# RWKV scan: inclusive decay sums only, decay products of both directions in one instruction, turned and unit blocks copied by ScalarE and GpSimd

## The chip, the cores and the metric

One Trainium2 chip, one of its cores. The metric is the device time in microseconds of one execution. The kernel before has a median of 3497.85 us over 3 runs (3496.07 to 3501.37). All data are float32; large products are made from high and low parts.

## The reference

Two transformer blocks of width 1024 on 1024 tokens. The first mixes with an RWKV-7 scan and a gated linear attention (GLA), each over half of the width, then an FFN and an embedding gate; the second mixes with neighbourhood attention and a convolution, then an MLP. The change is in the RWKV scan, which for each of 8 heads of 64 channels goes once forwards and once backwards over the tokens:

```python
def rwkv7_scan(r, decay, k, v, kk, b, reverse):
    def step(S, inp):                      # S: 64 x 64 for each head
        r_t, w_t, k_t, v_t, kk_t, b_t = inp
        sa = jnp.einsum('bhij,bhj->bhi', S, -kk_t)
        S = (S * w_t[:, :, None, :] + sa[..., None] * b_t[:, :, None, :]
             + v_t[..., None] * k_t[:, :, None, :])
        return S, jnp.einsum('bhij,bhj->bhi', S, r_t)
    ...
# decay = exp(-exp(-softplus(...) - 0.5)), that is exp(-exp(-0.5) * sigmoid(...))
y = (rwkv7_scan(r_h, heads(decay[:, :, 0]), k_h, v_h, kk, b_h, False)
     + rwkv7_scan(r_h, heads(decay[:, :, 1]), k_h, v_h, kk, b_h, True))
```

## The kernel before, in words

The program is written out engine by engine: each stage has one method per engine (`..._pe`, `..._act`, `..._dve`, `..._pool`, `..._sp`), each engine runs its instructions in the order written, and `wait_ge` makes an engine wait for a named count of another engine or of a transfer. Nothing is planned by a scheduler: the order in the methods is the order on the engines. `dve.c` stands for VectorE after a wait for its own last instruction.

The scan cuts the 1024 tokens into 16 chunks of 64 (NSUB), 8 blocks of two chunks (NBLK). A step handles one chunk of the forward direction (d = 0) and one of the backward direction (d = 1) at the same time, 4 pairs of heads each: 8 lanes, two heads on the two halves of the partitions. Within a chunk the recurrence is turned into products of matrices, for which a 64x64 triangular matrix has to be inverted for every head.

All engines run a loop over u from -2 to 15, software-pipelined: iteration u finishes chunk u, inverts for chunk m = u + 1 and prepares chunk n = u + 2, and VectorE makes the decay products of chunk u + 3. The pieces, by name:
- cum (TensorE, L1493): sums of the log decay of a block as a product with the constant `tri`, for even u up to 10. For every lane it gives 128 inclusive and 128 exclusive sums, in PSUM banks 2 and 3 of each direction; bank 2 also holds the right sides, bank 3 also ss.
- exps (ScalarE, L1609 to L1611): Ex, En and Ei, the exponentials of the exclusive sums, of the negative inclusive and of the inclusive sums.
- products (VectorE, L1700 to L1705), six instructions for each direction: F (the decay from chunk to chunk), AR and BK (kk, b, r and k times their decays), and the last decay kept for the next F.
- gb, gk (TensorE): the Gram matrices of BK and AR; masked into NM and MM by VectorE (L1720). tr (L1560): BK turned, copied to BKT by ScalarE (L1632).
- The inverse. VectorE inverts the 16x16 diagonal blocks by substitution in 15 steps on 32 partitions (`substitute_dve`, L1676 and L1677). NM goes to DRAM and its blocks come back as N16 (SP and GpSimd queues, L1427). Z16 holds the inverse at [:, :, 1], started as unit blocks (`identity_dve`, L1655) and turned to [:, :, 0] at the end (L1679, its mark is `x16`). Z16 goes to DRAM (L1459) and comes back as block diagonals ZZ: even blocks by SP, odd ones by GpSimd (L1436). Two levels then merge the blocks: p4 with ZZ, T (L1743), l4 (L1586, L1587), ZZ2 (L1747), p5, T (L1751), l5, XT (L1757). Of substitution n, steps 0 to 3 stand ahead of XT and steps 4 to 14 behind it.
- rh (`right_sides_pe`), copied with its sign changed to Rn by ScalarE (L1620); uu = XT times Rn, copied to U by ScalarE (L1623); ss and yy: the new state S and the output, both of which use U. VectorE adds ss into S (L1715) and scales it (L1725). y is written by ScalarE for u < 8 (L1628) and added by VectorE from then on (L1731).

In iterations with sums, rh stands behind l5, elsewhere ahead of p4. SP's order in its iteration n: NM to DRAM, ZZ blocks of n - 1, N16 blocks of n, the next sigmoids, Z16 to DRAM. GpSimd's: ZZ blocks of n - 1, N16 blocks of n. The helper that issues most of the products has one line (L1484), so a product is known by its tiles: ps<-s_AR,s_BK is gb or gk, ps<-s_ZZ,s_NM is p4, ps<-s_Rn,s_XT is uu.

Of the kernel before, what the change touches and what calls it, by code (L numbers as in the profile page):

```python
# [44 lines left out]
def constants():  # L45
# [6 lines left out]
    tri = np.zeros((2, PART, 2, PART), f)  # L52
    s, q = t[:, None], t[None, :]
    for d, (inc, exc) in enumerate((((s <= q), (s < q)), ((s >= q), (s > q)))):
        tri[d, :, 0] = DECAY * np.where(same, inc.astype(f) - 0.5, 0)
        tri[d, :, 1] = DECAY * np.where(same, exc.astype(f) - 0.5, 0)
    c["tri"] = np.ascontiguousarray(tri.transpose(1, 0, 2, 3)).reshape(PART, -1)
# [154 lines left out]
class Kernel:  # L212
# [116 lines left out]
    def plan_block1(self):  # L329
# [74 lines left out]
        self.tri, self.gram_mask, self.lev_mask = sb("tri", [PART, 2, 2 * PART]), sb("gram_mask", [PART, 2, 2, CH]), sb("lev_mask", [PART, 2, 2, CH])  # L404
        self.sig = sb("sig", [PART, 2, RW])
        self.Ei, self.En, self.Ex = (sb(n, [PART, LANES, PART]) for n in ("s_Ei", "s_En", "s_Ex"))
# [1032 lines left out]
    def rwkv_scan_sp(self):  # L1439
        sp, sg, pe, dve = self.sp, self.dram["sg"], self.pe, self.dve  # L1440
# [7 lines left out]
        for n in range(NSUB):  # L1448
# [9 lines left out]
            sp.wait_ge(dve["x16", n])  # L1458
# [5 lines left out]
        sp.wait_ge(dve["pr", NSUB - 1, 1])  # L1464
# [22 lines left out]
    def cum_pe(self, t):  # L1487

        pe = self.pe
        pe.wait_ge(self.t_in["sig", t])  # L1490
        for d in range(2):
            for x in range(4):
                mm = pe.e.matmul(self.ps[:, 4 * d + 2 + x // 2, (x % 2) * 256:(x % 2) * 256 + 256], self.sig[:, d, blk(x)], self.tri[:, d, :],  # L1493
                                 start=True, stop=True)
            mm.then_inc(*pe.one("cum", t, d))

    def right_sides_pe(self, u):
# [4 lines left out]
        for d in range(2):  # L1502
            pe.wait_ge(dve["scaled", u, d], self.pool["zero"])
            if (u % 2 or u == 0) and (u + 3) // 2 < NBLK:
                pe.wait_ge(act["Ei", (u + 3) // 2, d])
            elif u:
                pe.wait_ge(act["U", u - 1, d])
            if u:
                pe.wait_ge(self.yes(u - 1)["y", u - 1, d])
# [7 lines left out]
    def rwkv_scan_pe(self):  # L1517
        pe, act, dve, ps = self.pe, self.act, self.dve, self.ps
        for u in range(-2, NSUB):
# [6 lines left out]
            if n < NSUB:  # L1526
                AR_n = self.AR[n % 3]
                for w, name in ((0, "gb"), (1, "gk")):
                    for d in range(2):
                        pe.wait_ge(dve["pr", n, d])  # L1530
# [13 lines left out]
            elif u >= 0:  # L1544
                for d in range(2):
                    pe.wait_ge(act["U", u, d])
                    if u:
                        pe.wait_ge(dve["S", u - 1, d])
                    self.heads_pe(d, 3, CH, 0, ((lambda l, H: BKT[H, l, 1, :], v), (lambda l, H: BKT[H, l, 0, :], lambda l, H: self.U[H, l, :])), "ss", u, d)
# [13 lines left out]
            if sums:  # L1563
                if u >= 0:
                    pe.wait_ge(act["U", u, 1], self.yes(u)["y", u, 1], dve["S", u, 1])
                else:
                    pe.wait_ge(act["Ei", 0, 1])
                self.cum_pe((u + 4) // 2)
            elif 0 <= m < NSUB:
                self.right_sides_pe(m)  # L1570
            if 0 <= m < NSUB:
# [24 lines left out]
                if sums and m > 0:  # L1596
                    self.right_sides_pe(m)
        self.meet(pe, "rwkv_scan")

    def exps_act(self, t):  # L1600
# [3 lines left out]
        for d in range(2):  # L1604
            cum = ps[:, 4 * d + 2:4 * d + 4, :].rearrange("p b (l x t) -> p (b l) x t", l=2, x=2)
            act.wait_ge(pe["cum", t, d])
            if t:
                act.wait_ge(dve["pr", 2 * t - 1, d])
            act.e.activation(self.Ex[:, L[d]], cum[:, :, 1, :], ACTF.Exp).then_inc(*act.one())  # L1609
            act.e.activation(self.En[:, L[d]], cum[:, :, 0, :], ACTF.Exp, scale=-1.0).then_inc(*act.one())  # L1610
            act.e.activation(self.Ei[:, L[d]], cum[:, :, 0, :], ACTF.Exp).then_inc(*act.one("Ei", t, d))  # L1611

    def rwkv_scan_act(self):
        pe, act, dve, ps = self.pe, self.act, self.dve, self.ps
        L = [slice(0, 4), slice(4, 8)]
        for u in range(-2, NSUB):
            if u >= 0:
                for d in range(2):
                    act.wait_ge(pe["rh", u, d])
                    act.e.activation(self.Rn[:, L[d]], self.hb(d, 2), ACTF.Copy, scale=-1.0).then_inc(*act.one("Rn", u, d))  # L1620
                for d in range(2):
# [16 lines left out]
    def rwkv_scan_pool(self):  # L1638
        pool = self.pool
        pool.e.memset(self.S[0][:], 0.0).then_inc(*pool.one("zero"))  # L1640
        for n in range(NSUB + 1):
# [3 lines left out]
            if n < NSUB:  # L1645
                pool.wait_ge(self.t_n["out", n])
                self.blocks_there(pool, self.t_nb, n, range(5, 8))
        self.meet(self.pool, "rwkv_scan")

    def identity_dve(self, n):  # L1650

        dve = self.dve
        if n:
            dve.wait_ge(self.t_z["out", n - 1])
        dve.c.tensor_copy(self.Z16[:, :, 1], self.eye16[:]).then_inc(*dve.one("one", n))  # L1655

    def substitute_dve(self, n, first, end):
# [3 lines left out]
        if first == 0:  # L1661
            dve.wait_ge(dve["one", n])
# [6 lines left out]
        for s in range(first, end):  # L1669
# [7 lines left out]
            dve.c.tensor_tensor(rows, rows, part, ALU.subtract).then_inc(*dve.one())  # L1677
        if end == 15:
            dve.c.tensor_copy(self.Z16[:, :, 0], self.Z16[:, :, 1].rearrange("p d i c -> p d c i")).then_inc(*dve.one("x16", n))  # L1679

    def rwkv_scan_dve(self):
# [8 lines left out]
        def products(n, d):  # L1690
            t, AR, F = n // 2, self.AR[n % 3], self.F[n % 3]
            tok, s = self.gla_where(t, n % 2)[d]
            tc, W = slice(s * CH, (s + 1) * CH), slice(tok, tok + CH)
            last = s * CH + (CH - 1 if d == 0 else 0)
            dve.wait_ge(act["Ei", t, d])
            if n >= 3:
                dve.wait_ge(pe["yy", n - 3, d])
            if n:
                dve.wait_ge(pe["tr", n - 1, d])
            dve.c.tensor_tensor(F[:, L[d]], self.last[:, L[d]], self.Ei[:, L[d], last:last + 1], ALU.mult).then_inc(*dve.one())  # L1700
            dve.e.tensor_tensor(AR[:, L[d], 0], self.kk[:, :, W], self.Ex[:, L[d], tc], ALU.mult).then_inc(*dve.one())
# [1547 lines left out]
```

## Time and profile before

| | |
|---|---|
| median of 3 runs | 3497.85 us |
| profiled execution | 3500.24 us, its span 3498.9 us |
| scan, from the end of its second substitution to the end of its last | 752.1 to 1075.6 us of the span |
| TensorE busy | 3207.0 us, 92% |
| VectorE busy | 2220.8 us, 63% |
| ScalarE busy | 980.7 us, 28% |
| GpSimd busy | 459.9 us, 13% |
| granted TensorE clock, mean | 0.953 |

Busy time is the time in which an engine has an instruction at work; waits, semaphore and DMA-issuing instructions don't count. Matmuls overlap each other, and a row of a timeline joins like instructions that follow each other. The granted clock has two levels, 1.00 (2.4 GHz) and 0.50 (1.2 GHz). "Idle before <-releaser" is the time an engine stood still ahead of an instruction and what ended it.

### The profile page before, as it was taken

To read this page: it belongs to the slowest core of one execution; us is meant where nothing else is said; L and a number is where in the kernel's file an instruction comes from. 1 tells how busy PE (TensorE), PEld (TensorE's weight loads), DVE (VectorE), ACT (ScalarE), POOL (GpSimd) and SP (SyncE) were. 2 spreads that over 40 slices of the span, in tenths; PEclk is the share of its full clock that TensorE was granted. 3 is DMA by queue.
4 is the path that set the end of the run, shared out by engine and by line. 5 is a ranking of instruction groups with operands and counts; after the bars stand their busy time and mean duration, and the time that the engine had idled before them with its cause. 6 is when DMAs were issued, how large, how long until landed. Compare 5 with 4: busy or idle time off the path is not lost.

```text
span 3498.9 us, 58647 instructions
## 1 busy us (share of the span) xinstructions
PE 3207.0 (92%) x25755; PEld 2639.0 (75%) x25755; DVE 2220.8 (63%) x3060; ACT 980.7 (28%) x1514; POOL 459.9 (13%) x357
## 2 busy tenths in 40 slices
PE   6988888989987989999999887998998799999996
PEld 4777767778886878888888676885667688888885
DVE  4757655778886544444444566997546566666666
ACT  4544224322213221111111444112563211111112
POOL 2530023422224000000000121000001011111110
PEclk9988788999998999999999999999999899999999
DMA  4410044322224021111111212113001111111111
GB/s 128 127 63 11 20 134 139 118 40 42 40 31 171 7 67 37 55 55 37 55 55 42 80 42 73 49 43 99 2 2 61 42 49 49 49 49 49 49 49 66
DMA packets 242727, 207.41 MB, mean 59 GB/s; under 512 B 66744, under 2 KB 205127, under 8 KB 241959
## 3 DMA queue, kind: packets, MB, share of 16 engines
q1 hardware_dynamic: 223527, 176.96, 17.0%
q10 hardware_dynamic: 13824, 25.17, 2.3%
q0 software_dynamic: 5120, 1.53, 0.5%
q8 instruction: 202, 3.31, 0.4%
q14 instruction: 54, 0.44, 0.0%
HBM read 172.06 MB, written 29.64 MB: 58 GB/s over the span
## 4 chain that ended last, share of the span: by engine, by line
PE 69%; DVE 18%; ACT 5%; POOL 2%; DMA 2%; issue 2%; SPq 1%; ACTq 0%; DVEq 0%; POOLq 0%
PE ps L2176 23%; PE ps L2191 17%; PE ps L2038 5%; PE ps L640 3%; PE ps L641 3%; PE ps L642 3%; DVE Yc L2801 2%; PE ps L2900 2%; DVE s_tmp L1676 2%; DVE s_Z L1677 2%; PE ps L1484 1%; POOL a_x L2551 1%; PE ps L2926 1%; PE ps L2916 1%; PE ps L1012 1%
## 5 line engine op out<-in xcount | busy, mean ns | idle before, releaser
L3205 DVE TENSOR_TENSOR H<-H,ps 128x1024 f32<-128x1024 f32 x256 | 312.7, 1221 | 181.5 <-PE ps L2191 174.5
L2341 DVE TENSOR_TENSOR fsum<-fsum,ps 128x1024 f32<-128x1024 f32 x168 | 205.2, 1221 | 312.4 <-PE ps L2191 310.1
L2191 PE MATMUL ps<-dh,hh 128*128 128x512 f32 x864 | 340.1, 394 | 19.8 <-DVE hl L2156 13.9
L2191 PE MATMUL ps<-dl,hh 128*128 128x512 f32 x864 | 338.7, 392 | 0.0
L2191 PE MATMUL ps<-dh,hl 128*128 128x512 f32 x864 | 338.7, 392 | 0.0
L2176 PE MATMUL ps<-hn_h,uh 128*128 128x512 f32 x704 | 275.9, 392 | 7.2 <-DVE ul L1786 4.7
L2176 PE MATMUL ps<-hn_h,ul 128*128 128x512 f32 x704 | 275.4, 391 | 0.0
L2176 PE MATMUL ps<-hn_l,uh 128*128 128x512 f32 x704 | 275.4, 391 | 0.0
L2176 PE MATMUL ps<-hx_h,uh 128*128 128x512 f32 x512 | 201.4, 393 | 7.8 <-DVE hx_l L2156 5.3
L2191 PEld LDWEIGHTS ps<-dh,hh 128*128 128x128 f32 x864 | 163.9, 190 | 57.9 <-DVE hl L2156 15.5
L2176 PE MATMUL ps<-hx_h,ul 128*128 128x512 f32 x512 | 201.0, 393 | 0.0
L2176 PE MATMUL ps<-hx_l,uh 128*128 128x512 f32 x512 | 201.0, 393 | 0.0
L2191 PEld LDWEIGHTS ps<-dh,hl 128*128 128x128 f32 x864 | 163.7, 189 | 34.3
L2191 PEld LDWEIGHTS ps<-dl,hh 128*128 128x128 f32 x864 | 163.8, 190 | 33.7
L2551 POOL TENSOR_TENSOR a_x<-a_x,a_t 128x512 f32<-128x512 f32 x84 | 128.9, 1534 | 336.9 <-ACT a_t L2540 334.5
L3175 POOL TENSOR_TENSOR dw<-dw,g_row 128x1024 f32<-128x1024 f32 x32 | 78.7, 2461 | 708.5 <-DMA dw<-in_w_mlp_dram 708.5
L2176 PEld LDWEIGHTS ps<-hn_h,uh 128*128 128x128 f32 x704 | 133.1, 189 | 35.5 <-DVE ul L1786 5.2
L2801 DVE SCALAR_TENSOR_TENSOR Yc<-cp,cols,Yc 128x1024 f32<-128x1024 f32 x120 | 154.2, 1285 | 4.3
L2176 PEld LDWEIGHTS ps<-hn_l,uh 128*128 128x128 f32 x704 | 133.2, 189 | 27.7
L2176 PEld LDWEIGHTS ps<-hn_h,ul 128*128 128x128 f32 x704 | 133.0, 189 | 27.8
L3184 ACT ACTIVATE relu<-ps 128x1024 f32<-128x1024 f32 x32 | 32.9, 1030 | 404.4 <-PE ps L2176 404.4
L640 PE MATMUL ps<-hx_h,cw 128*128 128x512 f32 x320 | 129.7, 405 | 18.1 <-DVE cw L620 8.4
(473 smaller groups left out, 7412.3 us busy)
## 6 DMA issues: line engine op xcount, KB each, us to landing
aw<-in_w_ada_dram ACTq DMA_DIRECT2D x96, 256.0 KB, 3.0
uw<-in_w_mlp_dram SPq DMA_DIRECT2D x32, 512.0 KB, 4.4
dw<-in_w_mlp_dram SPq DMA_DIRECT2D x32, 512.0 KB, 5.2
uw<-in_ffn_gate_dram SPq DMA_DIRECT2D x22, 512.0 KB, 4.0
uw<-in_ffn_up_dram SPq DMA_DIRECT2D x22, 512.0 KB, 5.3
dw<-in_ffn_down_dram SPq DMA_DIRECT2D x22, 512.0 KB, 6.0
cw<-in_w_in_dram SPq DMA_DIRECT2D x20, 512.0 KB, 3.8
o_w<-in_w_out_dram SPq DMA_DIRECT2D x16, 512.0 KB, 10.0
```

The source lines that it names most:

```text
L640: pe.e.matmul(ps[0:m, 2 * (j % 2) + h, :], wh[:, k, :], xh, start=(k == 0), stop=False)
L641: pe.e.matmul(ps[0:m, 2 * (j % 2) + h, :], wh[:, k, :], xl, start=False, stop=False)
L642: mm = pe.e.matmul(ps[0:m, 2 * (j % 2) + h, :], wl[:, k, :], xh, start=False, stop=(k == kc - 1))
L1676: dve.c.tensor_tensor(part, col, pivot, ALU.mult).then_inc(*dve.one())
L2038: mm = pe.e.matmul(self.ps[:, 2 * (t % 2) + hf, :], x[a](k), w[b](k)[:, half(hf)], start=(n == 0 and m == 0), stop=(n == len(order) - 1 an ...
L2176: mm = pe.e.matmul(ps[:, 2 * pair + h, :], w[:, col], x[h][v][:, k, :], start=(k == 0 and m == 0), stop=(k == DC - 1 and m == 2))
L2191: mm = pe.e.matmul(ps[:, 2 * pair + hf, :], v[s][:, blk(t)], w[:, half(hf)], start=(m == 0), stop=(m == 2))
L2341: return dve.c.tensor_tensor(f, f, new, ALU.add) if g else dve.c.tensor_copy(f, new)
L2551: pool.c.tensor_tensor(acc[:], acc[:], self.a_t[who][:], ALU.add).then_inc(*pool.one("ada", q, who))
L2801: dve.c.scalar_tensor_tensor(out=o, in0=x[:, w:w + TOK], scalar=self.col("dw", n + 4 * w), in1=o, op0=ALU.mult, op1=ALU.add) \
L3175: pool.e.tensor_tensor(w, w, self.g2_row[:], ALU.mult).then_inc(*pool.one("m", "dw", g))
L3205: return dve.c.tensor_tensor(h, h, self.ps[:, 4 + 2 * (t % 2):6 + 2 * (t % 2), :], ALU.add)
```

## The change

- The exclusive sums are no longer computed: `tri` keeps 128 columns for each direction, cum fills bank 3 alone. The exclusive decay is the inclusive one of the token before: the exponentials go to a tile Eb of 65 columns for each chunk, with one edge column exp(-end) added. Ei and Ex are two views of Eb, shifted by one. ScalarE still has three activations for each direction, one of them with 8 columns.
- The products of both directions are made by one set of six instructions of 512 columns. The set waits for both directions' exps, yy and tr. Marks `pr` lose their direction.
- The turned copy of Z16 moves from VectorE to ScalarE (mark `x16`), between the Rn copies and the U copies of iteration u, for chunk u + 1; it waits for VectorE's mark `z16`, set by the last substitution step. The unit blocks move to GpSimd (mark `one`), between its ZZ and its N16 transfers.
- rh stands ahead of p4 in every iteration, and its wait for the exps (bank 2) goes to ss (bank 3). cum waits for S alone.

```diff
@@ -49,12 +49,8 @@
...
-    tri = np.zeros((2, PART, 2, PART), f)
     s, q = t[:, None], t[None, :]
-    for d, (inc, exc) in enumerate((((s <= q), (s < q)), ((s >= q), (s > q)))):
-        tri[d, :, 0] = DECAY * np.where(same, inc.astype(f) - 0.5, 0)
-        tri[d, :, 1] = DECAY * np.where(same, exc.astype(f) - 0.5, 0)
-    c["tri"] = np.ascontiguousarray(tri.transpose(1, 0, 2, 3)).reshape(PART, -1)
+    c["tri"] = np.concatenate([DECAY * np.where(same, inc.astype(f) - 0.5, 0) for inc in (s <= q, s >= q)], 1).astype(f)
@@ -401,9 +397,9 @@
...
         self.room = self.r0 + 112 * 1024
-        self.tri, self.gram_mask, self.lev_mask = sb("tri", [PART, 2, 2 * PART]), sb("gram_mask", [PART, 2, 2, CH]), sb("lev_mask", [PART, 2, 2, CH])
+        self.tri, self.gram_mask, self.lev_mask = sb("tri", [PART, 2, PART]), sb("gram_mask", [PART, 2, 2, CH]), sb("lev_mask", [PART, 2, 2, CH])
         self.sig = sb("sig", [PART, 2, RW])
-        self.Ei, self.En, self.Ex = (sb(n, [PART, LANES, PART]) for n in ("s_Ei", "s_En", "s_Ex"))
+        self.En, self.Eb = sb("s_En", [PART, LANES, 2, CH]), sb("s_Eb", [PART, LANES, 2, CH + 1])
@@ -1455,13 +1451,13 @@
...
                 sig((n + 3) // 2)
-            sp.wait_ge(dve["x16", n])
+            sp.wait_ge(act["x16", n])
             sp.e.dma_start(zd[n % 2].rearrange("k x d w i c -> (k x) (d w i c)"), self.Z16[:].rearrange("p d w i c -> p (d w i c)")) \
...
@@ -1490,8 +1486,7 @@
...
             for x in range(4):
-                mm = pe.e.matmul(self.ps[:, 4 * d + 2 + x // 2, (x % 2) * 256:(x % 2) * 256 + 256], self.sig[:, d, blk(x)], self.tri[:, d, :],
-                                 start=True, stop=True)
+                mm = pe.e.matmul(self.ps[:, 4 * d + 3, blk(x)], self.sig[:, d, blk(x)], self.tri[:, d, :], start=True, stop=True)
             mm.then_inc(*pe.one("cum", t, d))
@@ -1501,12 +1496,8 @@
...
             pe.wait_ge(dve["scaled", u, d], self.pool["zero"])
-            if (u % 2 or u == 0) and (u + 3) // 2 < NBLK:
-                pe.wait_ge(act["Ei", (u + 3) // 2, d])
-            elif u:
-                pe.wait_ge(act["U", u - 1, d])
             if u:
-                pe.wait_ge(self.yes(u - 1)["y", u - 1, d])
+                pe.wait_ge(act["U", u - 1, d], self.yes(u - 1)["y", u - 1, d])
             self.heads_pe(d, 2, CH, 0, ((lambda l, H: MM[H, l, 0, :], lambda l, H: self.VT[H, tok[l // 4], l % 4, :]),
@@ -1527,7 +1518,7 @@
...
                     for d in range(2):
-                        pe.wait_ge(dve["pr", n, d])
+                        pe.wait_ge(dve["pr", n])
                         if u >= 0:
@@ -1546,6 +1537,10 @@
...
                         pe.wait_ge(dve["S", u - 1, d])
+                    if u % 2 and (u + 3) // 2 < NBLK:
+                        pe.wait_ge(act["Ei", (u + 3) // 2, d])
+                    elif u == 0:
+                        pe.wait_ge(act["Ei", 1, d])
                     self.heads_pe(d, 3, CH, 0, ((lambda l, H: BKT[H, l, 1, :], v), (lambda l, H: BKT[H, l, 0, :], lambda l, H: self.U[H, l, :])), "ss", u, d)
@@ -1561,12 +1556,9 @@
...
             if sums:
-                if u >= 0:
-                    pe.wait_ge(act["U", u, 1], self.yes(u)["y", u, 1], dve["S", u, 1])
-                else:
-                    pe.wait_ge(act["Ei", 0, 1])
+                pe.wait_ge(dve["S", u, 1] if u >= 0 else act["Ei", 0, 1])
                 self.cum_pe((u + 4) // 2)
-            elif 0 <= m < NSUB:
+            if 0 <= m < NSUB:
                 self.right_sides_pe(m)
@@ -1593,8 +1585,6 @@
...
                     self.heads_pe(d, 1, CH, 0, ((lambda l, H: self.T[H, l, :], lambda l, H: ZZ2[H, l, 1, :]),), "l5", m, d)
-                if sums and m > 0:
-                    self.right_sides_pe(m)
         self.meet(pe, "rwkv_scan")
@@ -1602,13 +1592,14 @@
...
         for d in range(2):
-            cum = ps[:, 4 * d + 2:4 * d + 4, :].rearrange("p b (l x t) -> p (b l) x t", l=2, x=2)
+            cum = ps[:, 4 * d + 3, :].rearrange("p (l s t) -> p l s t", l=4, s=2)
+            inc, edge, end = (slice(1, CH + 1), slice(0, CH))[d], (slice(0, 1), slice(CH, CH + 1))[d], (slice(CH - 1, CH), slice(0, 1))[d]
             act.wait_ge(pe["cum", t, d])
             if t:
-                act.wait_ge(dve["pr", 2 * t - 1, d])
-            act.e.activation(self.Ex[:, L[d]], cum[:, :, 1, :], ACTF.Exp).then_inc(*act.one())
-            act.e.activation(self.En[:, L[d]], cum[:, :, 0, :], ACTF.Exp, scale=-1.0).then_inc(*act.one())
-            act.e.activation(self.Ei[:, L[d]], cum[:, :, 0, :], ACTF.Exp).then_inc(*act.one("Ei", t, d))
+                act.wait_ge(dve["pr", 2 * t - 1])
+            act.e.activation(self.Eb[:, L[d], :, inc], cum, ACTF.Exp).then_inc(*act.one())
+            act.e.activation(self.Eb[:, L[d], :, edge], cum[:, :, :, end], ACTF.Exp, scale=-1.0).then_inc(*act.one())
+            act.e.activation(self.En[:, L[d]], cum, ACTF.Exp, scale=-1.0).then_inc(*act.one("Ei", t, d))
@@ -1618,6 +1609,10 @@
...
                     act.e.activation(self.Rn[:, L[d]], self.hb(d, 2), ACTF.Copy, scale=-1.0).then_inc(*act.one("Rn", u, d))
+            if 0 <= u + 1 < NSUB:
+                act.wait_ge(dve["z16", u + 1])
+                act.e.activation(self.Z16[:, :, 0], self.Z16[:, :, 1].rearrange("p d i c -> p d c i"), ACTF.Copy).then_inc(*act.one("x16", u + 1))
+            if u >= 0:
                 for d in range(2):
@@ -1643,23 +1638,18 @@
...
             if n < NSUB:
+                pool.wait_ge(self.t_misc["r_const"])
+                pool.e.tensor_copy(self.Z16[:, :, 1], self.eye16[:]).then_inc(*pool.one("one", n))
                 pool.wait_ge(self.t_n["out", n])
...
-    def identity_dve(self, n):
-        dve = self.dve
-        if n:
-            dve.wait_ge(self.t_z["out", n - 1])
-        dve.c.tensor_copy(self.Z16[:, :, 1], self.eye16[:]).then_inc(*dve.one("one", n))
     def substitute_dve(self, n, first, end):
...
         if first == 0:
-            dve.wait_ge(dve["one", n])
+            dve.wait_ge(self.pool["one", n])
             dve.wait_ge(self.t_n["in", n], self.t_nb["in", n])
@@ -1674,9 +1664,7 @@
...
             dve.c.tensor_tensor(part, col, pivot, ALU.mult).then_inc(*dve.one())
-            dve.c.tensor_tensor(rows, rows, part, ALU.subtract).then_inc(*dve.one())
-        if end == 15:
-            dve.c.tensor_copy(self.Z16[:, :, 0], self.Z16[:, :, 1].rearrange("p d i c -> p d c i")).then_inc(*dve.one("x16", n))
+            dve.c.tensor_tensor(rows, rows, part, ALU.subtract).then_inc(*(dve.one("z16", n) if s == 14 else dve.one()))
@@ -1687,25 +1675,35 @@
...
-        def products(n, d):
-            t, AR, F = n // 2, self.AR[n % 3], self.F[n % 3]
-            tok, s = self.gla_where(t, n % 2)[d]
-            tc, W = slice(s * CH, (s + 1) * CH), slice(tok, tok + CH)
-            last = s * CH + (CH - 1 if d == 0 else 0)
-            dve.wait_ge(act["Ei", t, d])
+        def both(x, y):
+            return bass.AP(tensor=x.tensor, offset=x.offset, ap=[x.ap[0], [y.offset - x.offset, 2]] + list(x.ap[1:]))
+        def products(n):
+            t, AR, BK, F = n // 2, self.AR[n % 3], self.BK, self.F[n % 3]
+            (tok, s), (tok_b, s_b) = self.gla_where(t, n % 2)
+            W, W_b = slice(tok, tok + CH), slice(tok_b, tok_b + CH)
+            def decays(at, at_b):
+                return both(self.Eb[:, L[0], s, at:at + CH], self.Eb[:, L[1], s_b, at_b:at_b + CH])
+            def lanes(x):
+                return x.rearrange("p (d x) t -> p d x t", d=2)
+            Ei, Ex, En = decays(1, 0), decays(0, 1), both(self.En[:, L[0], s], self.En[:, L[1], s_b])
+            end = both(self.Eb[:, L[0], s, CH:CH + 1], self.Eb[:, L[1], s_b, 0:1])
+            dve.wait_ge(act["Ei", t, 0], act["Ei", t, 1])
             if n >= 3:
-                dve.wait_ge(pe["yy", n - 3, d])
+                dve.wait_ge(pe["yy", n - 3, 1])
             if n:
-                dve.wait_ge(pe["tr", n - 1, d])
-            dve.c.tensor_tensor(F[:, L[d]], self.last[:, L[d]], self.Ei[:, L[d], last:last + 1], ALU.mult).then_inc(*dve.one())
-            dve.e.tensor_tensor(AR[:, L[d], 0], self.kk[:, :, W], self.Ex[:, L[d], tc], ALU.mult).then_inc(*dve.one())
-            dve.e.tensor_tensor(self.BK[:, L[d], 0], self.bb[:, :, W], self.En[:, L[d], tc], ALU.mult).then_inc(*dve.one())
-            dve.e.tensor_tensor(AR[:, L[d], 1], rkv[:, 0:4, W], self.Ei[:, L[d], tc], ALU.mult).then_inc(*dve.one())
-            dve.e.tensor_tensor(self.BK[:, L[d], 1], rkv[:, 4:8, W], self.En[:, L[d], tc], ALU.mult).then_inc(*dve.one())
-            dve.c.tensor_copy(self.last[:, L[d]], self.Ei[:, L[d], last:last + 1]).then_inc(*dve.one("pr", n, d))
-        for d in range(2):
-            products(0, d)
+                dve.wait_ge(pe["tr", n - 1, 1])
+            dve.c.tensor_tensor(lanes(F[:]), lanes(self.last[:]), end, ALU.mult).then_inc(*dve.one())
+            dve.e.tensor_tensor(lanes(AR[:, :, 0]), both(self.kk[:, :, W], self.kk[:, :, W_b]), Ex, ALU.mult).then_inc(*dve.one())
+            dve.e.tensor_tensor(lanes(BK[:, :, 0]), both(self.bb[:, :, W], self.bb[:, :, W_b]), En, ALU.mult).then_inc(*dve.one())
+            dve.e.tensor_tensor(lanes(AR[:, :, 1]), both(rkv[:, 0:4, W], rkv[:, 0:4, W_b]), Ei, ALU.mult).then_inc(*dve.one())
+            dve.e.tensor_tensor(lanes(BK[:, :, 1]), both(rkv[:, 4:8, W], rkv[:, 4:8, W_b]), En, ALU.mult).then_inc(*dve.one())
+            dve.c.tensor_copy(lanes(self.last[:]), end).then_inc(*dve.one("pr", n))
+        products(0)
         for u in range(-2, NSUB):
@@ -1732,11 +1730,8 @@
...
                     self.rwkv_rk_dve(c)
-            for d in range(2):
-                if u + 3 < NSUB:
-                    products(u + 3, d)
-            if n < NSUB:
-                self.identity_dve(n)
+            if u + 3 < NSUB:
+                products(u + 3)
             if 0 <= m < NSUB:
```

## Rows read from the trace of the kernel before

**Rows 1.** The page: span, and each engine's busy time, share and instructions.

```profile
span 3498.9 us, 58647 instructions
...
PE 3207.0 (92%) x25755; PEld 2639.0 (75%) x25755; DVE 2220.8 (63%) x3060; ACT 980.7 (28%) x1514; POOL 459.9 (13%) x357
```

**Rows 2.** Windows, core 0: stretch, length, busy of PE, PEld, DVE, ACT, POOL, clock, DMA.

```profile
752.10:1075.60 323.50, 293.18 (x7694) 276.69 (x7689) 266.53 (x841) 63.22 (x136) 83.96 (x140) 0.98 0.22 37
870.80:872.70 1.90, 0.09 (x4) 0.03 (x2) 1.75 (x7) 0.38 (x1) 1.90 (x4) 1.00 0.26 19
873.40:876.70 3.30, 3.30 (x68) 3.30 (x64) 1.54 (x3) 0.00 (x0) 0.00 (x0) 0.50 0.63 164
```

**Rows 3.** Chain of waits, 700 to 1100: start us, length us, what.

```profile
752.13 0.60 DVE s_Z L1679
...
888.33 0.61 DVE s_Z L1679
...
891.30 0.53 SPq L1436
...
897.07 0.71 PE ps L1484 x16
...
911.44 0.62 DVE s_Z L1679
...
1075.59 0.58 DVE s_Z L1679
...
1078.29 4.78 DVE r_rkv L1917 x4
1083.08 0.44 DVE s_T L1743
```

**Rows 4.** PE's waits, 752.1 to 1075.6: us in total, times, longest.

```profile
PE ps L1484 <- DMA s_ZZ<-zd_dram: 14.3, 11, 2.2
```

**Rows 5.** Timeline of ScalarE: start, length, instruction, [idle before <-releaser].

```profile
748.02 0.85 ACT L1623 ACTIVATE s_U<-ps 128x256 f32<-128x256 f32 x2 [10.13 <-PE ps L1484]
...
884.22 0.85 ACT L1623 ACTIVATE s_U<-ps 128x256 f32<-128x256 f32 x2 [12.94 <-PE ps L1484]
...
908.99 0.85 ACT L1623 ACTIVATE s_U<-ps 128x256 f32<-128x256 f32 x2 [3.58 <-PE ps L1484]
...
914.51 0.38 ACT L1628 ACTIVATE B<-ps 128x256 f32<-128x256 f32 x1 [1.02 <-PE ps L1484]
...
916.38 0.60 ACT L1632 ACTIVATE s_BKT<-ps 128x512 f32<-128x512 f32 x1 [0.34 <-PE ps L1560]
...
918.24 0.38 ACT L1620 ACTIVATE s_Rn<-ps 128x256 f32<-128x256 f32 x1 [0.55 <-PE ps L1484]
...
1069.82 0.85 ACT L1623 ACTIVATE s_U<-ps 128x256 f32<-128x256 f32 x2 [11.21 <-PE ps L1484]
```

**Rows 6.** Timeline of TensorE.

```profile
872.67 0.51 PE L1484 MATMUL ps<-s_ZZ,s_NM 64*64 64x64 f32 x10 [1.81 <-DMA s_ZZ<-zd_dram]
...
892.27 3.72 PE L1493 MATMUL ps<-tri,sig 128*128 128x256 f32 x16
```

**Rows 7.** Timeline of VectorE.

```profile
881.28 0.73 DVE L1757 TENSOR_TENSOR s_XT<-s_ZZ,ps 128x256 f32<-128x256 f32 x2
...
889.53 1.27 DVE L1720 TENSOR_TENSOR s_NM<-ps,gram_mask 128x512 f32<-128x512 f32 x2
...
892.80 0.17 DVE L1700 TENSOR_TENSOR s_F<-s_last,s_Ei 128x4 f32<-128x4 f32 x1
...
896.43 0.41 DVE L1655 COPY s_Z<-eye 32x512 f32<-32x512 f32 x1
```

**Rows 8.** Groups by line and form, GpSimd, whole span: xcount | busy us, mean ns | idle.

```profile
L2551 POOL TENSOR_TENSOR a_x<-a_x,a_t 128x512 f32<-128x512 f32 x84 | 128.9, 1534 | 336.9 <-ACT a_t L2540 334.5
...
L1640 POOL MEMSET s_S<- 128x512 f32 x1 | 0.5, 524 | 11.8 <-DVE s_last L1685 11.8
```

More of the change, by code:

```diff
@@ L1439, in rwkv_scan_sp @@
     def rwkv_scan_sp(self):
-        sp, sg, pe, dve = self.sp, self.dram["sg"], self.pe, self.dve
+        sp, sg, pe, act, dve = self.sp, self.dram["sg"], self.pe, self.act, self.dve
         nd, zd = self.dram["nd"], self.dram["zd"]
@@ L1463, in rwkv_scan_sp @@
         i = self.i
-        sp.wait_ge(dve["pr", NSUB - 1, 1])
+        sp.wait_ge(dve["pr", NSUB - 1])
         for dst, src in ((self.r_hones[:], i["k_head_ones"]), (self.r_hsel2[:], i["k_head_sel"]), (self.r_gup[:], i["rwkv_g_up"][0]),
```

## The prediction

> **What bounds the kernel now.** I read the page first: TensorE is busy 92% of the span and VectorE 63% [rows 1]. These shares are averages over stages, so next came a stretch of the scan alone, between the ends of its second and last substitution: in 323.5 us TensorE is busy 293, VectorE 267, ScalarE 63 [rows 2]. Neither of the first two is saturated, so the step is set by a loop, and I took the chain of waits to see it [rows 3]. I mark a step by E, the start of the copy at L1679, which is the end of the 15 substitution steps. From E = 888.33 VectorE copies (L1679), adds S, masks NM; the SP queue issues the return of the inverted blocks at 891.30; p4 (the first product with ZZ) starts at 897.07, so 8.7 us after E; from there p4, T, l4, ZZ2, p5, T, l5, XT and eleven substitution steps reach the next E at 911.44, 14.37 us later. The first marked E is 752.13, the last 1075.59: 14 periods of 23.1 us [rows 3]. TensorE's waits for the returned blocks are only 14.3 us over the stage [rows 4]: transfer, VectorE's filling work and TensorE end almost together, so taking work from one of them can give little, and holding one of them up costs at once.
>
> ScalarE looks free (63 us of 323), but what matters is when its few instructions are due. U of the step is copied at 884.22, 4.1 us before E, and in the steps with decay sums at 908.99, 2.4 us before E; the first U is at 748.02 (E 752.13), the fifteenth at 1069.82 (E 1075.59) [rows 3, 5]. U comes before E in every step.
>
> **The change, part by part.**
>
> *The turned copy goes to ScalarE, and this is the term that decides.* In the new ScalarE program of iteration u the order is Rn(u), turn x16(u+1), U(u). The turn waits for z16(u+1). VectorE's iteration u-1 ends with substitution n = u+1, so z16(u+1) is exactly the E ahead of which U(u) is copied now. ScalarE takes its instructions in order: U(u) can't start until E. Queued behind U(u) are ss(u) and yy(u) on TensorE (L1549 and the line of yy behind it), behind them tr(u+2), the sums, the right sides and p4; and on VectorE S(u) waits for ss(u), with NM, MM, products and all transfers of the next step behind it. Fifteen U (u = 0 to 14) are held.
>
> I place the new step from E on. ScalarE sees E 0.1 us later. The 32x512 turn: 0.60 us is what a 128x512 activation takes (the BKT row), the 128x256 ones take 0.38, VectorE needed 0.61 for this copy [rows 3, 5]; bounds 0.4 to 1.1 (twice the 512-column row, less overlap, for its strided read); I take 0.5 until the next one issues, so U starts at E+0.6. From a U, the rows of 908.99 to 918.24 give what TensorE does with no wait: second y copy 5.52 later, second BKT 7.39, second Rn 9.25 [rows 5]. So tr is done at E+8.0 and the right sides at E+9.85.
> - Steps with sums (u = 0, 2, ... 10: six). The sums take 3.72 us now for 16 matmuls of 256 columns [rows 6]; with 128 columns between 1.86 and 3.72, I take 1.86, as time per matmul here goes with columns. The right sides now stand ahead of p4 in these steps too. p4 at 9.85 + 1.86 = E+11.7.
> - Steps without (eight of the fourteen periods). TensorE is ready at E+9.85, and the returned blocks decide. ss is two fifths of the matmuls between U and the second y copy, so about 0.45 + 2.0 us: S of the second direction starts at E+3.0, NM is done 0.33 + 1.2 later [rows 7], E+4.5. SP sends NM first and then its half of the ZZ blocks, so the issue at 891.30 (E+3.0 now) moves to E+5.0; now p4 follows that issue by 5.77 us [rows 3], in other steps by 5.0. p4 at E+10.0 to 10.8; I take 10.6.
> From p4 to the next E nothing is changed: 14.37. Periods at full clock: 26.1 and 25.0. Six and eight of them: 356.6 us against 323.5, so **+33**. The last step: y of both directions now waits for U(14), E+6.5, and L1917 (4.78 us) follows: T at E+11.4 where it was 1083.08 - 1075.59 = E+7.5; +3.9, with the clock below **+4.8**.
>
> *TensorE's clock.* From the end of uu (the second of the two U copies of 884.22 starts about 3.7 us before E) to E+1.05 TensorE would now have nothing: 4.7 us in every step. In the trace it waits 1.81 us for a transfer up to 872.67 (0.09 us busy in 870.8 to 872.7), and the stretch 873.4 to 876.7 then has a granted clock of 0.50, which is 1.2 of 2.4 GHz [rows 2, 6]. That period needs 15.66 us from p4 (872.67) to E and not 14.37 [rows 3, 6]. The mean clock of the scan is 0.98, so some 13 us lie at the lower level: about four such stretches. I take one of 3.3 us per step. Between U and p4 all is TensorE's work, so it costs half of it, 1.65 us: steps with sums 27.75. In the others the products end later: tr 9.65, products 2.9 (below) to 12.55, T can start then instead of 0.73 after p4, equal to a p4 at 11.8: 26.2. Six and eight: 376.1, which is **+52.6** instead of +33. The Trainium skill (TensorE: Matmul & The Clock Gate, "HAM oscillation — how this bites in real kernels") says that a wait that returns in every iteration makes the clock fall in every iteration. By that rule the clock's 20 us are in the sum; by a reading in which falls stay as rare as in this trace the sum would be +37. The single fall shown follows a wait of less than half the new one, and so far agrees with the rule.
>
> *Products of both directions at once.* Twelve instructions take 892.80 to 896.43, 3.63 us [rows 7]. Now six: four of 128x512 at the 0.60 us pitch of NM (two in 1.27), the two small ones and their drains 0.5: 2.9. If the four-level patterns cost nothing extra this saves 0.7; if they ran at half that rate it would cost 1.7 more. The set now waits for the second tr, E+8.0, while VectorE is free from E+6.4: the saving is hidden by that wait.
>
> *Copies off VectorE.* The turn (0.61) and the unit blocks (0.41 at 896.43 [rows 7]) leave VectorE. On the path the turn is replaced by ScalarE's, about +0.1; the unit blocks lay beside the transfer. VectorE is relieved of 1.7 us per step in a place where it would now wait for ss and tr: nothing gained. On GpSimd the copy has bounds of 0.52 us (memset 128x512) and 1.53 (two-input 128x512) [rows 8]. It stands behind four ZZ issues (E+3 to E+5.2) and ahead of the N issues, whose data is at E+7.5: hidden; without that cover, at most 1.5 us before a substitution that starts 16 us after E.
>
> *The exps* stay six per block, two of them small; ScalarE has room for them between the products and Rn. The wait of rh on them moves to ss of an earlier step, where they are long done. Start of the scan: one shorter set of sums and fewer VectorE instructions, **-1**.
>
> **Sum.** +52.6 + 4.8 - 1 = +56. The profiled execution took 3500.24 us (span 3498.9), so 3556.6; the median of the runs is 2.4 lower, so **3554**.
>
> **Rivals.**
> 1. *The same blocking, the clock doesn't fall more often than now.* For: TensorE's other short waits passed without a fall. Against: the 1.81 us one. +33 + 3.9 - 1: 3534. Chance 0.17.
> 2. *Two low stretches per step.* For: the wait is longer than one such stretch. Against: TensorE works without a gap for nine microseconds after it. 14 x 1.65 more: 3578. Chance 0.17.
> 3. *Faster: VectorE sets the step.* For: it is busy 267 of 323 us, the substitutions fill the chain [rows 2, 3], and 1.7 us per step leave it. Then 15 x 1.7 = 26 us go: 3472. It decides from the point where the turn is ready when uu is, that is where substitution ends less than 3 us after XT; XT starts at 881.28 and E is 888.33, 7 us later [rows 3, 7]. Chance 0.04.
> 4. *The change does not relieve anything, and U's wait is hidden in TensorE's slack*: no change, 3498. It would need 5 us of slack where the trace shows 14.3 us in all [rows 4]. Chance 0.02.
> 5. *Combined products at half rate, with the blocking*: products end some 2.4 us later, mostly beyond the right sides, about 1.5 us on the eight steps without sums and less on the others: 3570. Chance 0.05.
>
> **Numbers.** Forecast 0.55. The range 3526 to 3590 takes in rivals 1, 2 and 5, the early end of the returned blocks (0.6 us on eight steps) and a turn of 1.1 us (0.5 us on fifteen). A change of under 0.2% (7 us) is what a measurement of this kernel can't tell from none: faster 0.04, within 0.02, slower 0.94.
>
> **What would show it.** ScalarE's U should start right behind the turned copy, both just after the last substitution, in fifteen steps; TensorE should show an idle of 4 to 5 us ahead of ss, released by U, fifteen times; VectorE an idle of about 2 us ahead of S and 1.5 us ahead of F. E to E should be 25 to 28 us, longer with sums. Granted clock of the scan clearly under 0.98. The sums at 1.9 us. It is wrong if U still leads E, if ss starts without a wait, or if the period stays at 23.

## The result, and the profile after

The changed kernel has a median of 3569.84 us over 4 runs (3562.6 to 3575.37) against 3499.2 us over 4 runs of the kernel before: ratio 1.0199, 95% interval 1.018 to 1.0217, so 70.6 us slower. The forecast was 3554 in 3526 to 3590, 56 us slower. The profiled execution took 3575.37 us, span 3573.7.

The page after, the rows that answer to [rows 1]. The span grew by 75 us; TensorE is busy 18 us longer, VectorE 23 us less and the others have hardly moved, so most of what was added is waiting.

```profile
span 3573.7 us, 58522 instructions
## 1 busy us (share of the span) xinstructions
PE 3225.1 (90%) x25755; PEld 2662.1 (74%) x25755; DVE 2197.4 (61%) x2932; ACT 985.2 (28%) x1530; POOL 468.1 (13%) x373
```

The windows after (stretch, length, then busy time of PE, PEld, DVE, ACT and POOL, granted clock, DMA share, GB/s). The first is the scan from the end of its second substitution to the end of its last, the answer to the first of [rows 2]; the other two are the wait for U in one step and what follows it.

```profile
759.10:1143.30 384.20, 300.40 (x7648) 287.60 (x7648) 246.48 (x735) 67.75 (x150) 91.84 (x154) 0.89 0.18 31
895.10:900.20 5.10, 0.12 (x6) 0.00 (x0) 3.33 (x14) 1.28 (x3) 0.00 (x0) 1.00 0.01 3
900.20:903.60 3.40, 3.31 (x61) 3.31 (x63) 0.42 (x1) 0.30 (x2) 1.40 (x3) 0.51 0.20 41
```

The same fourteen periods now take 384.2 us and took 323.5. VectorE has 20 us less to do there. TensorE is busy 7 us more although its sums are shorter, because it runs at the lower clock more often: a mean of 0.89 for 0.98.

TensorE's waits in that stretch (us in total, times, longest), which answer to [rows 4]: the returned blocks have left the head of the list, and U is new in it, once in every period.

```profile
PE ps L1480 <- ACT s_U L1618: 71.0, 14, 5.1
PE ps L1480 <- DVE s_ZZ L1742: 3.5, 14, 0.3
```

The timeline of ScalarE for one step, against [rows 5], and of TensorE. ScalarE stands idle for 12.1 us until the last substitution step is done, then makes the turned copy (L1614), and U (L1618) starts behind it. TensorE works on uu from 894.13 to 895.23 and then stands until 900.29.

```profile
898.92 1.06 ACT L1614 ACTIVATE s_Z<-s_Z 32x512 f32<-32x512 f32 x1 [12.14 <-DVE s_Z L1667]
899.88 0.62 ACT L1618 ACTIVATE s_U<-ps 128x256 f32<-128x256 f32 x2
```

```profile
894.13 1.10 PE L1480 MATMUL ps<-s_Rn,s_XT 64*64 64x64 f32 x32
...
900.29 0.49 PE L1480 MATMUL ps<-s_VT,s_BKT 64*64 64x64 f32 x4 [5.07 <-ACT s_U L1618]
```

The timeline of VectorE in the same step, against [rows 7]: it waits for ss, and again for the second tr ahead of F; T follows the products at once, so in this step, one without sums, the products are what comes last ahead of T.

```profile
902.36 0.42 DVE L1713 TENSOR_TENSOR s_S<-s_S,ps 128x256 f32<-128x256 f32 x1 [3.48 <-PE ps L1480]
903.97 0.42 DVE L1713 TENSOR_TENSOR s_S<-s_S,ps 128x256 f32<-128x256 f32 x1 [1.19 <-PE ps L1480]
...
908.97 0.17 DVE L1699 TENSOR_TENSOR s_F<-s_last,s_Eb 128x8 f32<-128x8 f32 x1 [1.52 <-PE ps L1555]
...
911.67 0.75 DVE L1738 TENSOR_TENSOR s_T<-ps,lev_mask 128x256 f32<-128x256 f32 x2
```

The chain of waits over one step without sums (start, length, what), against [rows 3], where the transfer and SP stood between the substitution and p4. They are gone from the chain; ScalarE's turn, U and a row of TensorE's work took their place.

```profile
898.92 1.06 ACT s_Z L1614
899.98 0.27 ACT s_U L1618
900.29 6.46 PE ps L1480 x158
906.87 1.75 PE ps L1555 x60
908.97 0.17 DVE s_F L1699
...
911.76 0.34 DVE s_T L1738
...
925.29 1.06 ACT s_Z L1614
```

### The profile page after: what moved, and what is told of

The parts are those of the page before. It is cut to its first block, busy times and chain, and to the rows that moved or that the text cites. A ratio compares the mean times of both kernels' runs of the same rounds, so it can differ in the third digit from the quotient of the medians.

```text
span 3573.7 us, 58522 instructions
## 1 busy us (share of the span) xinstructions
PE 3225.1 (90%) x25755; PEld 2662.1 (74%) x25755; DVE 2197.4 (61%) x2932; ACT 985.2 (28%) x1530; POOL 468.1 (13%) x373
## 4 chain that ended last, share of the span: by engine, by line
PE 72%; DVE 16%; ACT 6%; POOL 2%; issue 2%; DMA 1%; SPq 0%; ACTq 0%; DVEq 0%; POOLq 0%
PE ps L2171 23%; PE ps L2186 16%; PE ps L2033 5%; PE ps L1480 4%; PE ps L636 3%; PE ps L637 3%; PE ps L638 3%; DVE Yc L2796 2%; DVE s_tmp L1666 2%; DVE s_Z L1667 2%; PE ps L2895 2%; POOL a_x L2546 1%; PE ps L2921 1%; PE ps L2911 1%; PE ps L1008 1%
```

## Experiments

E is again the end of a substitution, read from the start of the turned copy. The fourteen periods from the second E to the last are given for each; they are 323.5 us before and 384.2 after. They come from one profile of each kernel, the times from all its runs.

**U ahead of the turn.** The edit to the changed kernel, in ScalarE's loop:

```diff
+            if u >= 0:
+                for d in range(2):
+                    act.wait_ge(pe["uu", u, d])
+                    act.e.activation(self.U[:, L[d]], ...)
             if 0 <= u + 1 < NSUB:
                 act.wait_ge(dve["z16", u + 1])
                 act.e.activation(self.Z16[:, :, 0], ...)
-            if u >= 0:
-                for d in range(2):
-                    ...
```

> The changed kernel with one edit: on ScalarE the U copies stand ahead of the turned copy of Z16. Theory (U is held behind the turn, and TensorE behind U): U starts 4 us before the end of the substitution again, TensorE's wait of 5 to 7 us ahead of ss is gone, the period falls from 27.4 to about 23, and the time to 3485 to 3505 us. Rival 1 (the loss comes from the rest: combined products that wait for the second tr, the turn's 1.06 us on the way to the transfer, GpSimd's copy): the time stays above 3545 us. The fraction of 70 us that stays is what the rest costs.

Measured: 3497.8 us, ratio to the kernel before 0.999 (0.9973 to 1.0007). Fourteen periods 320.7 us. Its timeline of ScalarE has U 4.1 us before the turn, as in [rows 5], and in the list of TensorE's waits over its fourteen periods U is gone:

```profile
903.84 0.85 ACT L1615 ACTIVATE s_U<-ps 128x256 f32<-128x256 f32 x2 [7.95 <-PE ps L1480]
907.95 1.09 ACT L1618 ACTIVATE s_Z<-s_Z 32x512 f32<-32x512 f32 x1 [3.27 <-DVE s_Z L1667]
```

The whole loss hangs on the order of two instructions. Everything else of the change together is worth nothing in this kernel that can be told from zero.

**The turn back on VectorE.** The changed kernel with L1679 of the kernel before restored and the ScalarE copy removed.

> The changed kernel with the turned copy back on VectorE; sums, products, order of the right sides and GpSimd's unit blocks as in the changed kernel. Theory: no instruction of ScalarE waits for the substitution, so 3480 to 3500 us; against the kernel with U ahead of the turn it differs by 0.6 us on VectorE for 1.06 us on ScalarE, some 0 to 6 us lower if the way to the transfer ends the wait. Rival 1: above 3545 us, since all other parts are kept.

Measured: 3498.07 us, ratio 0.9982 (0.997 to 0.9995). Fourteen periods 317.2 us. It confirms the same thing by another way: the loss is gone with the turn off ScalarE. The interval lies just below 1, so this kernel may be 2 to 10 us faster than the one before.

**The turn alone, on the kernel before.**

```diff
+            if 0 <= u + 1 < NSUB:
+                act.wait_ge(dve["z16", u + 1])
+                act.e.activation(self.Z16[:, :, 0], self.Z16[:, :, 1].rearrange("p d i c -> p d c i"), ACTF.Copy).then_inc(*act.one("x16", u + 1))
+            if u >= 0:
                 for d in range(2):
                     act.wait_ge(pe["uu", u, d])
```

> The kernel before with one part of the change alone: the turned copy on ScalarE between the Rn and U copies. Theory: it carries the whole loss, 3555 to 3580 us, with TensorE waiting for U fifteen times. Rival 1: the turn costs only its longer duration on the way to the transfer, 15 x 0.5 us, so 3505 to 3510 us.

Measured: 3566.5 us, ratio 1.0184 (1.0169 to 1.0199), periods 381.4 us, the clock of that stretch 0.92. TensorE's wait for U, in the stretch 753 to 1134 of this kernel:

```profile
PE ps L1484 <- ACT s_U L1627: 60.9, 14, 5.1
```

One part of the change carries the loss: 1.0184 of 1.0199, with overlapping intervals.

**TensorE kept at work while it waits.** The changed kernel with products between uu and ss whose results nobody reads:

```diff
+            if 0 <= u < NSUB - 1:
+                for k in range(4):
+                    for d in range(2):
+                        ...
+                        self.heads_pe(d, 3, CH, 256, ((lambda l, H: XT[H, l, :], lambda l, H: self.Rn[H, l, :]),), "fill", u, d)
```

> The changed kernel with eight more sets of products of XT and Rn (four per direction) between uu and ss, into a part of PSUM that nobody reads, so that TensorE works while it waits for U. Theory with the clock as second term: granted clock of the scan from 0.89 to over 0.97, the period from 27.4 to 25.5 us, 3535 to 3550 us. Rival 2 (the wait alone costs, the clock is a side effect that the path hides): the period stays at 27 and the time within 5 us of 3570, or above where the added products run past U.

Measured: 3544.64 us, ratio 1.0124 (1.0109 to 1.0139): 25 us less than the changed kernel, with 1920 more matmul instructions in the stage and U as late as there, 0.97 us after E. The window of its fourteen periods (columns as above), and its wait for U:

```profile
752.40:1110.90 358.50, 326.96 (x9442) 314.08 (x9440) 246.33 (x734) 67.71 (x150) 91.87 (x154) 1.00 0.20 34
```

```profile
PE ps L1480 <- ACT s_U L1628: 18.7, 14, 1.3
```

The clock is 1.00, and the periods are 26.5 us with sums and 24.6 to 25.5 without. TensorE still waits 1.3 us for U in a step, so the added products don't run past it. This parts the loss of the fourteen periods in two: 358.5 - 323.5 = 35 us is the blocking itself, 384.2 - 358.5 = 26 us is the clock that falls because of the waiting. The medians of the two kernels differ by 25 us as well. The 35 us hang on single profiles, and those of the kernels without the blocking range from 313.0 to 323.5 us.

**The other parts one by one.** On the kernel before, the products of both directions in one set; and the inclusive sums alone, with the right sides ahead of p4:

```diff
-            for d in range(2):
-                if u + 3 < NSUB:
-                    products(u + 3, d)
+            if u + 3 < NSUB:
+                products(u + 3)
```

> The kernel before with one part alone: products of both directions in one set of six instructions. Theory: the set takes 2.9 us for 3.6 and begins once the second tr is done; it lies beside the transfer, so 0 to -5 us: 3494 to 3500 us. Rival: gb has to wait for both directions and the transfer is not hidden as well, +2 to +8 us.

Measured: 3498.39 us, ratio 1.0003 (0.999 to 1.0017). Fourteen periods 314.0 us. No difference from the kernel before is shown, and the interval holds most of both expectations.

```diff
-                mm = pe.e.matmul(self.ps[:, 4 * d + 2 + x // 2, ...], self.sig[:, d, blk(x)], self.tri[:, d, :], ...)
+                mm = pe.e.matmul(self.ps[:, 4 * d + 3, blk(x)], self.sig[:, d, blk(x)], self.tri[:, d, :], start=True, stop=True)
```

> The kernel before with the inclusive sums alone (with Eb and the right sides ahead of p4 in every step; products by direction, turn and unit blocks on VectorE). Theory: the sums take 1.9 to 2.0 us for 3.7 in seven steps and the right sides move to a place where TensorE waits for the transfer: -3 to -8 us, 3491 to 3497 us. Rival: the sums were hidden behind the transfer, within 2 us of the kernel before.

Measured: 3498.39 us, ratio 0.9997 (0.9986 to 1.0008). Fourteen periods 319.4 us. The expected gain of 3 to 8 us is not shown: the interval reaches from 5 us faster to 3 slower, so a small gain within it can't be excluded either. The sums do get shorter: they take 2.05 us for 3.72.

**How the turn is read.** U first, with the stride on the written side, and U first, with a plain copy:

```diff
-                act.e.activation(self.Z16[:, :, 0], self.Z16[:, :, 1].rearrange("p d i c -> p d c i"), ACTF.Copy)...
+                act.e.activation(self.Z16[:, :, 0].rearrange("p d i c -> p d c i"), self.Z16[:, :, 1], ACTF.Copy)...
```

> The changed kernel with U ahead of the turn, and the turn made by a write with stride instead of a read with stride. Theory (the read with a step of 64 bytes is what makes the 32x512 activation 1.06 us long): the turn takes about 0.6 us and the time falls by up to 15 x 0.45 = 7 us against the read with stride. Rival: 1.06 us stays, either because writing with stride costs the same or because ScalarE takes this long from SBUF: same time as the kernel with U first.

Measured: 3495.92 us, ratio 0.9992 (0.9981 to 1.0003). Fourteen periods 315.3 us. My theory of the read falls: the copy takes as long with the stride on the written side.

> The changed kernel with U ahead of the turn, and a plain copy in place of the turned one on ScalarE (the blocks that come back are therefore not turned). Theory: the step of 64 bytes on one side is what makes the 32x512 activation 1.06 us long, and the plain one takes about 0.6 us. Rival: ScalarE takes 1.06 us for 512 columns from SBUF whatever the pattern. The time says nothing beyond 15 x 0.45 us.

Measured: 3490.49 us in its one run, fourteen periods 313.0 us. The turn's group (count, busy us, mean ns, idle before) with the read turned, with the write turned, and plain:

```profile
L1618 ACT ACTIVATE s_Z<-s_Z 32x512 f32<-32x512 f32 x16 | 17.4, 1088 | 59.8 <-DVE s_Z L1667 59.8
```

```profile
L1618 ACT ACTIVATE s_Z<-s_Z 32x512 f32<-32x512 f32 x16 | 17.4, 1089 | 60.4 <-DVE s_Z L1667 60.4
```

```profile
L1618 ACT ACTIVATE s_Z<-s_Z 32x512 f32<-32x512 f32 x16 | 10.1, 630 | 60.4 <-DVE s_Z L1667 60.4
```

The turn costs ScalarE 0.46 us over a plain copy, on whichever side the stride is.

**Unit blocks later.** On the kernel with the turn on VectorE, GpSimd's copy behind its N16 transfers:

```diff
-                pool.e.tensor_copy(self.Z16[:, :, 1], self.eye16[:]).then_inc(*pool.one("one", n))
                 pool.wait_ge(self.t_n["out", n])
                 self.blocks_there(pool, self.t_nb, n, range(5, 8))
+                pool.e.tensor_copy(self.Z16[:, :, 1], self.eye16[:]).then_inc(*pool.one("one", n))
```

> The changed kernel with the turn on VectorE, and GpSimd's unit blocks moved behind its transfers of the N blocks. Theory (a product of VectorE with two operands in SBUF stands still while GpSimd copies within SBUF: 1.10 for 0.69 us): the products are 0.69 us each again, 0.4 us per step come back where VectorE is late, 0 to -6 us against the turn on VectorE, so 3486 to 3496 us. Rival: they lie beside the transfer, no change: 3493 to 3498 us.

Measured: 3495.52 us, ratio 0.9988 (0.9977 to 0.9998), fourteen periods 319.0 us. The products are 0.69 us each again, but the time can't be told from that of the kernel without the move (0.9982, 0.997 to 0.9995). This fits the rival, by which they lay beside the transfer.

**A candidate: three queues for the returned blocks.**

```diff
-                self.inverse_back(sp, self.t_z, n - 1, range(0, 8, 2))
+                self.inverse_back(sp, self.t_z, n - 1, range(0, 5, 2))
...
-                self.inverse_back(pool, self.t_zb, n - 1, range(1, 8, 2))
+                self.inverse_back(pool, self.t_zb, n - 1, range(1, 6, 2))
...
+            if 0 <= u + 1 < NSUB:
+                act.wait_ge(self.t_z["out", u + 1], self.pool["zero"])
+                self.inverse_back(act, self.t_zc, u + 1, range(6, 8))
             if u + 2 < NSUB:
                 for d in range(2):
                     act.wait_ge(pe["tr", u + 2, d])
```

> The kernel with the turn on VectorE and late unit blocks, and the return of the ZZ blocks spread over three queues: SP 3, GpSimd 3, ScalarE 2 (ahead of its BKT copies) where it was 4 and 4. Theory (the path from E to p4 is the transfer, and its issues are 0.5 us each in a row): the last issue is 0.5 us earlier, 15 x 0.5 = 7 us off where the transfer ends the wait, 3483 to 3493 us. Rival: the landing is set by the transfer engines and not by the issues, or ScalarE's BKT copies come late: 3493 to 3500 us.

Measured: 3493.0 us, ratio 0.9988 (0.9976 to 1.0). The ratio is that of the kernel it was built on (0.9988), so no gain of the third queue is shown. Its fourteen periods are 314.3 us, but the combined products alone had 314.0 in their profile with a ratio of 1.0003: single profiles of this stage differ by as much as was to be shown. The clock is a part of that scatter. Read in windows of 0.25 us, there are at the lower level 13.6 us of the fourteen periods of the kernel before, 20.5 us with U first and none with the combined products alone. All versions without the blocking that compute the same as the kernel before lie within 0.2% of its time; none is clearly better than it by more than that.

## Why the prediction was right

**The deciding step.** U(u) behind the turn of u + 1: as put, in all 15 steps, with TensorE's idle released by U (71.0 us in 14 periods, 5.1 each; foretold 4.7; the fifteenth is 6.7 us). VectorE's waits are there: 3.5 us ahead of S, where about 2 were foretold, and 1.5 ahead of F. The experiments on the order alone (0.999) and on the turn alone (1.0184) show that this step is the cause, and the only one of a size that these runs can tell.

**The blocking at full clock.** Foretold 356.6 us for fourteen periods and 3.9 more for the last step. The run with the filled TensorE gives 358.5, in periods of 26.5 with sums and 25.0 on average without, against 26.1 and 25.0.

**The turn on ScalarE was mis-sized.** I took 0.5 us until U issues, from a 128x512 activation, with 1.1 as the far bound; it is 0.96, because the turned pattern makes the copy 1.06 us long. A plain copy would have been 0.63. The doubt that I noted (its stride) was the right one, and I chose by the row nearest in shape and not by the one nearest in pattern, of which there was none. At full clock the miss shows in the six steps with sums: p4 starts at E+12.1 in the filled run, where E+11.7 was foretold. In the steps without sums it is hidden by another miss. I had the returned blocks decide there, with p4 at E+10.6 and T at E+11.3. In five of these eight steps of the filled run the blocks are earlier than the products, and T starts right behind the products at E+11.2, as in the step of E = 881.47:

```profile
892.61 0.21 DVE L1714 COPY s_last<-s_Eb 128x8 f32<-128x8 f32 x1
892.69 0.75 DVE L1748 TENSOR_TENSOR s_T<-ps,lev_mask 128x256 f32<-128x256 f32 x2
```

So at full clock the period without sums came out right by luck. With the clock's stretch added I had put the products last, and there the changed kernel agrees: T at E+12.6 to 12.8 in half of these steps, where E+12.55 was foretold.

**The clock.** This is the largest miss. Foretold 20 us (one low stretch of 3.3 us in each step); measured 26 us by the filled run. Read in windows of 0.25 us, 82.6 of the 384.2 us lie at the lower level, in one unbroken stretch per step. In five of the fourteen steps it lasts 3.4 us and stands behind the wait for U, as in the step shown above (900.2 to 903.6). In the other nine it lasts 6.8 us and begins while TensorE still waits. The step of E = 925.29 has the latter (columns as above):

```profile
921.70:924.20 2.50, 0.00 (x0) 0.00 (x0) 2.19 (x10) 0.00 (x0) 0.00 (x0) 0.99 0.00 0
924.20:926.60 2.40, 0.00 (x0) 0.00 (x0) 0.92 (x5) 1.31 (x3) 0.00 (x0) 0.50 0.00 0
926.60:931.10 4.50, 4.43 (x82) 4.44 (x84) 1.09 (x3) 0.28 (x2) 2.53 (x5) 0.51 0.23 40
```

What falls in the wait costs nothing. TensorE works in 57.3 of the 82.6 us, 4.1 us per step where I took 3.3, and half of 57.3, 29 us, is an estimate of the cost, near the 26 us measured. Rival 2 (two low stretches in each step) had their length nearly right for nine steps, but counted all of it as work: 24 us more than the forecast, where the runs show six. Rival 1 (no more falls than before) is refuted: the kernel before had four stretches, the changed one has one in every step. The rule of the Trainium skill (TensorE: Matmul & The Clock Gate, "HAM oscillation — how this bites in real kernels"), that a wait in every iteration brings the fall in every iteration, agrees with this trace: a mean clock of 0.89 for 0.98, and 1.00 once the wait was filled.

**The sum by its terms**, in the two profiled executions (span 74.8 us longer, the medians 70.6):

| | foretold | measured |
|---|---|---|
| fourteen periods | +52.6 | +60.7 |
| last step, from E to the end of L1917's four (L1912 in the changed kernel) | +4.8 | +6.3 |
| start of the scan | -1 | +2.4 |
| stages ahead of the scan | 0 | +4.6 |

Of the 8.1 us that the periods lie above the forecast, 6.2 are the clock and 1.9 the blocking.

The fourth is no part of the change: the scan's first instruction starts at 710.77 and not 706.16, in stages whose code is the same, and in the profiles of the experiments, with the same stages ahead, the first E lies anywhere from 724.7 to 737.6 us. The third had a sign that I missed: with one set for both directions, the very first gb waits for all six instructions instead of one direction's six short ones, 3.5 us after the scan's first instruction and not 2.0. That is 1.5 us; the rest stays open.

**The parts costed at nothing** hold within the intervals: the saving of the products is hidden (1.0003), VectorE's relief buys nothing that shows (0.999 with the turn on ScalarE in the right place), and moving the unit blocks on GpSimd changes nothing (0.9982 and 0.9988). The sums were nearly right in duration (1.98 us in the changed kernel's chain of waits for 1.86). Rival 3, that VectorE sets the step, is refuted: with U first VectorE's work in the stage fell from 267 to 250 us, and the time by 3 us, at most 9 by its interval, where this rival had 26.

What stays open is whether the rest of the change gains some 5 us: its kernels' ratios lie between 0.9982 and 1.0003 with intervals 0.2% to 0.3% wide. Two of these intervals end just below 1 (0.9995 and 0.9998, both with the turn on VectorE), so a small gain may well be there, but it isn't sized.

## What to carry to other kernels

Before an instruction is moved to an engine that looks idle, write down when what it waits for is ready and when the instruction behind it is due now: a 1 us copy on an engine that is 28% busy cost 70 us, because in each of 15 steps it waited some 4 us past the point at which its successor was needed. Put the one that waits longest last among those that are ready together. And where a wait is added to TensorE in every iteration, ask what the clock loses: here 26 us on top of 35, counting only the part of the low stretch in which TensorE has work.

## What the runs showed of the hardware

VectorE and GpSimd get in each other's way. With the turn on VectorE the GpSimd copy of unit blocks (SBUF to SBUF) meets a product of VectorE with both operands in SBUF. The two timelines of that kernel:

```profile
875.11 0.69 DVE L1700 TENSOR_TENSOR s_BK<-r_bb,s_En 128x512 f32<-128x512 f32 x1
875.71 1.10 DVE L1701 TENSOR_TENSOR s_AR<-r_rkv,s_Eb 128x512 f32<-128x512 f32 x1
876.73 0.68 DVE L1702 TENSOR_TENSOR s_BK<-r_rkv,s_En 128x512 f32<-128x512 f32 x1
```

```profile
875.57 0.69 POOL L1639 COPY s_Z<-eye 32x512 f32<-32x512 f32 x1
```

The product that overlaps the copy takes 1.10 us where its neighbours take 0.69; with the copy moved away all four kinds have means of 684 to 686 ns, and the copy takes 0.62 us for 0.69. In the changed kernel the copy falls beside the masks, which have one input in PSUM, and neither is longer: the copy takes 0.62 us, and two masks 1.28 us where they took 1.27. The Trainium skill (SBUF — State Buffer, "Who interferes with whom") says that a VectorE instruction with two SBUF inputs contends with a GpSimd instruction that reads SBUF; the traces agree, with 0.4 us in a step. The prediction has no term for it, and the run with the copy moved away shows that none was needed here.

A ScalarE copy of 32x512 between SBUF tiles takes 0.63 us plain and 1.09 us with steps of 64 bytes on either side; VectorE takes 0.60 us for the same turned copy and 0.43 us for the plain copy of the unit blocks in the kernel before.
